# Rotary keys: the weights' high and low parts side by side in one stationary operand, their halves added on VectorE

## The chip, the cores and the metric

One Trainium2 chip, one core of it. A core has TensorE (matrix products into PSUM), VectorE, ScalarE and GpSimd, and 16 DMA engines between HBM and the on-chip SBUF; each engine runs its own list of instructions in order, and they wait for each other on semaphores. The metric is the device time of one execution in microseconds; a kernel's time is the median over its runs.

## The reference

Two blocks on 512 tokens of 1024 channels, in fp32. The first is attention with latent keys, a Fourier branch and experts; the second a recurrent unit and a feed-forward layer. The change touches one small piece of the first block:

```
h  = rms(x, norm1_g) * (1 + sc) + sh          # 512 tokens
hc = rms(ctx, norm1_g) * (1 + csc) + csh      # 256 context tokens
p, pc = h @ w_in, hc @ w_in
k_pe  = p[..., OFF_KPE:OFF_F]                 # 32 rotary columns, one for all heads
k = concat([k_nope, k_pe repeated over heads])
k = rms(k, k_norm_g)                          # mean square over all 96, so k_pe's squares count
k = concat([k[:64], rope(k[64:])])            # latent tokens only
```

So of the 32 rotary key rows three things are wanted: their values, times k_norm_g, and the sum of their squares per token (before k_norm_g).

## The kernel before, in words

Everything is kept with channels on the 128 partitions and tokens along the free axis. Products are made exact enough by splitting each fp32 operand in a high part (fp32r, a rounded copy, made on ScalarE) and a low part (the rest, made on VectorE or, for weights, on GpSimd), and doing three products: high x high, high x low, low x high. That is mm3 (L961 to L963); project (L968) repeats it over the 8 channel blocks of 128. Each such product is one instruction of up to 512 tokens, with its own load of the stationary weights.

Weights come as pieces of 128x2048 through a ring of four raw buffers. ScalarE copies a piece to w_hi (split_weights, L1704, called from take() when the piece is due by the plan), then GpSimd makes w_lo (L895), then the raw buffer is filled again. Three pieces are held in w_hi and w_lo. The weights of the rotary keys, 8 blocks of 32 columns, lie in the third piece of the section "s1".

The order is written out by hand, in one list per engine. PLAN lists the PSUM tiles in the order in which TensorE fills them, with a bank and with who frees each. Around the change, TensorE does:

1. cq and ckv for the 512 tokens (L1078), then rope_rows(0) (L1106): the tile "kpe" 0, 32 rows x 512 tokens, 8 x 3 products;
2. ckv_c for the 256 context tokens (two halves, 48 products), which waits for hc_lo; then rope_rows(1), the tile "kpe" 1, 32 rows x 256;
3. fourier_in(0); then the sums over channels of all squares into the tile ssq_c, as products of one column (L1013 for cq and ckv, L1131 for the rotary keys, the latter after act_seq 3);
4. fourier_in(1); the broadcasts of the inverse norms (L1020); rot_k (L1143), a rotation of the scaled keys, which waits for both "kpe" tiles to be freed; then the rest of the Fourier branch.

ScalarE, in order: hc_hi for 8 blocks (L1714, each waits for VectorE's pre), dftc_hi (L1761), the squares of cq and ckv (L1765), of ckv_c, and of the two "kpe" tiles (L1774, into sqk), then f_hi of the Fourier tiles. VectorE: pre and hc_lo (L2152, L2160), the gains of cq and ckv (L2186, L2201) with the sums of their squares between (L2191), ckv_c, the two "kpe" tiles times k_norm_g into kraw (L2212), f_lo of tile 0 (L2219), then the copy of the key sums (L2222), the inverse norms (L2123 to L2135, some 14 small steps), f_lo of tile 1.

Of the kernel before, what the change touches and what calls it, by code (L numbers as in the profile page):

```python
# [4 lines left out]
F32 = mybir.dt.float32  # L5
F32R = mybir.dt.float32r
I32 = mybir.dt.int32
U32 = mybir.dt.uint32
ALU = mybir.AluOpType
ACT = mybir.ActivationFunctionType  # L10
AX = mybir.AxisListType

P = 128
T = 512
TC = 256
TK = T + TC
D = 1024
KD = D // P
EPS = 1e-6
H = 8  # L20
QK = 96
NOPE = 64
ROPE = 32
VD = 64
QL = 384 // P
KL = 256 // P
# [15 lines left out]
CH = 2048  # L42
NRAW = 4
NHL = 3
# [8 lines left out]
S1_QKV, S1_KPE, S1_F, S1_DFT = 0, 44 * B, 46 * B, 80 * B  # L53
# [28 lines left out]
COLS = {}  # L82
# [102 lines left out]
SPLIT0 = {s: section_start(s, True) for s, _, sp in SECTIONS if sp}  # L185
# [272 lines left out]
PLAN = make_plan()  # L458
TILE = PLAN.tiles
# [29 lines left out]
def build(nc, stream, cols_d, x_d, ctx_d, router_d, wab_d, rope_d, rope_t_d, rot_d, dftc_d, ident_d, iota_d, xt_d, out):  # L489
    with ExitStack() as ctx:  # L490
        base = 16512

        def at(name, kb, shape, dt=F32):
            return nc.alloc_sbuf_tensor_at(name, shape, dt, offset=base + int(kb * 1024))

        def sem(name):
            return ctx.enter_context(nc.semaphore(name))
# [3 lines left out]
        w_hi = at("w_hi", 32, [P, NHL, CH], F32R)  # L501
        w_lo = at("w_lo", 56, [P, NHL, CH], F32R)
        ex_ring = at("ex_ring", 0, [P, NEX - 1, CH])
        R = 80

        x1 = at("x1", R + 96, [P, KD, T])
        cols = at("cols", R + 122.75, [P, NCOLS])
# [35 lines left out]
        ckvg = at("ckvg", R + 54, [P, KL, TK])  # L543
        sq_q = at("sq_cq", R + 60, [P, QL, T])
        sq_kv = at("sq_ckv", R + 66, [P, KL, TK])
# [10 lines left out]
        kraw = at("kraw", R + 104, [QK, TK])  # L556
        sqk = at("sqk", R + 107, [QK, TK])
        rk = at("rk", R + 110, [QK, T])
        rope_t = at("rope_t", R + 112, [P, 2 * TT + 2, ROPE])
        kr_tok = at("kr_tok", R + 113.25, [P, KT, ROPE])  # L560
        rope_cs = at("rope_cs", R + 115, [QK, 2, T])
# [114 lines left out]
        w_lo_done = sem("w_lo_done")  # L676
# [5 lines left out]
        freed_dve = sem("freed_dve")  # L682
# [6 lines left out]
        macc_done = sem("macc_done")  # L689
        modb_done = sem("modb_done")  # L690
        latent_sums = sem("latent_sums")
        modin_full = [sem(f"modin_full{i}") for i in range(KD)]
        x_in = [sem(f"x_in{i}") for i in range(4)]
        ctx_in = sem("ctx_in")
# [3 lines left out]
        sq_done = sem("sq_done")  # L698
# [5 lines left out]
        act_seq = sem("act_seq")  # L704
# [64 lines left out]
        def col(name, j=0, n=1):  # L769
            return cols[:, COLS[name] + j:COLS[name] + j + n]  # L770

        def bank(*name):
            return psum[:, PLAN.bank[TILE[name]], :]

        def full(eng, *name):

# [154 lines left out]
        def _(pe):  # L931
            mm = nc.tensor.matmul
            seen = [0]

            def open_tile(*name):

                t = TILE[name]
                prev = PLAN.prev[t]
                if prev is not None:
                    pe.wait_ge(freeing[PLAN.freed[prev][0]], PLAN.freed_count(prev))  # L940
                return psum[:, PLAN.bank[t], :]
# [23 lines left out]
            def done(ins):  # L965
                ins.then_inc(tile_full, 1)

            def project(o, base, off, width, ks, x_of):  # L968

                for i, k in enumerate(ks):  # L970
                    last = mm3(o, weights(base, off + i * width, width), x_of(k), i == 0, i == len(ks) - 1)
                return last
# [70 lines left out]
            o = open_tile("ssqx_rows")  # L1043
            for j in range(KD):
                pe.wait_ge(sq_done, j // 2 + 1)
                last = row_sums(o, sq_x0, j)
# [6 lines left out]
            o = open_tile("bc_x")  # L1053
# [6 lines left out]
            s1 = SPLIT0["s1"]  # L1060
            hx = lambda k: (h_hi[:, k, :], h_lo[:, k, :])
            hcx = lambda k: (hc_hi[:, k, :], hc_lo[:, k, :])
# [12 lines left out]
            ks = range(KD)  # L1075
# [8 lines left out]
            for k in range(KD):  # L1084
                for i in range(QL + KL):
                    last = qkv_step(i, k)
# [18 lines left out]

            def rope_rows(s):  # L1106

                o = open_tile("kpe", s)
                done(project(o[0:ROPE, 0:TC if s else T], s1, S1_KPE, ROPE, ks, hcx if s else hx))

            rope_rows(0)
            o = open_tile("ckv_c")
# [26 lines left out]
            done(broadcast(o3[2], 2 * TT, 2))  # L1139

            o = open_tile("rot_k")
            pe.wait_ge(freed_dve, PLAN.freed_count(TILE["kpe", 1]))
            done(mm(o[0:QK, :], rotm[NOPE:QK, :], kraw[NOPE:QK, 0:T], start=True, stop=True))  # L1143
            fourier_in(2)
            fourier_in(3)
# [541 lines left out]
        def _(act):  # L1687
# [19 lines left out]
            def take(*name):  # L1707

                split_weights(TILE[name])
                full(act, *name)  # L1710
                return bank(*name)
# [52 lines left out]
            def square(dst, src):  # L1764
                A(dst, src, ACT.Square).then_inc(sq_done, 1)  # L1765

            for j in range(QL):
                square(sq_q[:, j, :], take("cq", j))
            for j in range(KL):
                square(sq_kv[:, j, 0:T], take("ckv", j))  # L1770
            square(sq_kv[:, :, T:TK], take("ckv_c").rearrange("p (j t) -> p j t", j=KL))
            for s in range(2):
                w = slice(T, TK) if s else slice(0, T)
                A(sqk[NOPE:QK, w], take("kpe", s)[0:ROPE, 0:w.stop - w.start], ACT.Square).then_inc(act_seq, 1)  # L1774
            hi(f_hi[:, 0, :], take("f", 0))
            hi(f_hi[:, 1, :], take("f", 1))
            for j in range(QL):
# [282 lines left out]
        def _(dve):  # L2060
# [3 lines left out]
            def link(ins):  # L2064

                n[0] += 1
                ins.then_inc(dve_seq, 1)
                dve.wait_ge(dve_seq, n[0])
# [8 lines left out]
            def take(*name):  # L2077
                full(dve, *name)
                return bank(*name)

            def free(ins):
                ins.then_inc(freed_dve, 1)
# [107 lines left out]
            def latent_sum(dst, src):  # L2190
                V.tensor_tensor(dst, dst, src, ALU.add).then_inc(latent_sums, 1)  # L2191
                sums[0] += 1
                dve.wait_ge(latent_sums, sums[0])
# [6 lines left out]
                dve.wait_ge(sq_done, nsq)  # L2200
                free(V.tensor_scalar(ckvg[:, j, 0:T], o, col("kv_a_norm_g", j), None, ALU.mult))  # L2201
            latent_sum(sq_kv[:, 0, 0:T], sq_kv[:, 1, 0:T])
            o = take("ckv_c")
            dve.wait_ge(sq_done, nsq + 1)
            V.tensor_scalar(ckvg[:, 0, T:TK], o[:, 0:TC], col("kv_a_norm_g", 0), None, ALU.mult)
            free(V.tensor_scalar(ckvg[:, 1, T:TK], o[:, TC:T], col("kv_a_norm_g", 1), None, ALU.mult))
            latent_sum(sq_kv[:, 0, T:TK], sq_kv[:, 1, T:TK])
            for s in range(2):
                w = slice(0, T) if s == 0 else slice(T, TK)
                o = take("kpe", s)  # L2210
                dve.wait_ge(act_seq, 2 + s)
                free(V.tensor_scalar(kraw[NOPE:QK, w], o[0:ROPE, 0:TC if s else T],  # L2212
                                     cols[NOPE:QK, COLS["k_norm_g"]:COLS["k_norm_g"] + 1], None, ALU.mult))
            dve.wait_ge(freed_dve, PLAN.freed_count(TILE["kpe", 1]))

            def evac_lo(dst, hi_part, *name):
                o = take(*name)
                dve.wait_ge(hi_done, SPLITS[name] + 1)
                V.tensor_tensor(dst, o, hi_part.bitcast(F32), ALU.subtract).then_inc(lo_done, 1)  # L2219

            evac_lo(f_lo[:, 0, :], f_hi[:, 0, :], "f", 0)
            link(V.tensor_copy(kpe_s, take("ssq_c")[:, TT + KT:TT + 2 * KT]))  # L2222
            inverse_norms(take("ssq_c"), 10, [(0, 4, 1.0 / (QL * P)), (4, 6, 1.0 / (KL * P))])
            evac_lo(f_lo[:, 1, :], f_hi[:, 1, :], "f", 1)
# [670 lines left out]
```

## Time and profile before

| | us |
|---|---|
| median of 3 runs | 1335.6 |
| lowest, highest | 1334.64, 1336.63 |
| span of the profiled execution | 1332.2 |
| its TensorE busy | 1313.8 |
| its mean granted TensorE clock (share of full speed) | 0.996 |

The profile shows one execution; its span runs from the first to the last instruction, and the profiled execution's own time is not listed apart from it. Times in the trace count from the span's start. In a timeline each row has the start, how long the instruction or a run of them was busy, the engine, the line, output<-input, shapes, and the count; in square brackets how long the engine was idle before it and who released it. "128*32" is a stationary operand of 128 rows and 32 columns. Products are pipelined, so the durations of neighbours overlap: the distance between starts is what one costs.

### The profile page before, as it was taken

The page shows a single profiled execution, that of the slowest core. Times are in us where ns is not written, and L with a number is a line of the kernel's source. Part 1 is how long each engine was busy: PE and PEld are TensorE (multiplying, and loading weights), DVE is VectorE, ACT ScalarE, POOL GpSimd, SP SyncE. Part 2 cuts the span into 40 slices and gives each one's busy share as a digit, 9 for nine tenths or more (in the row PEclk, how much of TensorE's full clock was granted, in tenths as well). Part 3 has the DMA queues.
Part 4 walks back from the last instruction along what each step waited for, and adds up shares of the span by engine and source line. Part 5 has one row for each costly group of instructions (what it writes and reads, how often), then busy time and mean ns, then how long its engine had stood idle before and what let it go on. Part 6 is the DMA issues. An engine that isn't in the chain of part 4 may idle for free.

```text
span 1332.2 us, 15820 instructions
## 1 busy us (share of the span) xinstructions
PE 1313.8 (99%) x6366; PEld 966.9 (73%) x6366; DVE 690.1 (52%) x1261; ACT 461.6 (35%) x618; POOL 433.8 (33%) x136
## 2 busy tenths in 40 slices
PE   8999999999999899999999999999999999999998
PEld 6789888865587834343457788888888888888887
DVE  2465987757783733343356656612562551551553
ACT  4335223345621221121135571433341431431431
POOL 3143244247612000000015333444245344444440
PEclk9999999999999899999999999999999999999999
DMA  9521198201025799999983122222132223123101
GB/s 378 214 96 64 58 356 336 103 1 64 32 96 189 294 375 421 421 421 420 421 367 127 63 80 110 96 95 95 63 126 98 93 95 118 71 94 126 64 1 64
DMA packets 34501, 226.70 MB, mean 170 GB/s; under 512 B 4064, under 2 KB 4704, under 8 KB 8448
## 3 DMA queue, kind: packets, MB, share of 16 engines
q1 hardware_dynamic: 32992, 218.93, 42.9%
q0 software_dynamic: 1152, 4.19, 0.8%
q10 hardware_dynamic: 288, 2.62, 0.5%
q8 instruction: 48, 0.79, 0.2%
q14 instruction: 21, 0.17, 0.0%
HBM read 221.53 MB, written 4.19 MB: 169 GB/s over the span
## 4 chain that ended last, share of the span: by engine, by line
PE 94%; DVE 3%; DMA 1%; ACT 1%; SPq 0%; issue 0%; DVEq 0%; ACTq 0%
PE psum L961 24%; PE psum L963 23%; PE psum L962 23%; PE psum L1465 13%; DMA mod_in<-in_stream 1%; PE psum L1273 1%; PE psum L1239 1%; PE psum L1450 1%; PE psum L1453 1%; PE psum L1008 1%; PE psum L1537 1%; PE psum L1425 1%; PE psum L1674 1%; DVE rs L2381 1%; PE psum L1013 0%; DVE work L2512 0%
## 5 line engine op out<-in xcount | busy, mean ns | idle before, releaser
L895 POOL TENSOR_TENSOR w_lo<-raw,w_hi 128x2048 fp32r<-128x2048 f32 x79 | 365.3, 4627 | 589.9 <-ACT w_hi L1704 589.9
L961 PE MATMUL psum<-b_hi,w_hi 128*128 128x512 f32 x608 | 238.1, 392 | 0.1
L963 PE MATMUL psum<-b_hi,w_lo 128*128 128x512 f32 x608 | 236.7, 389 | 0.0
L962 PE MATMUL psum<-b_lo,w_hi 128*128 128x512 f32 x608 | 236.6, 389 | 0.0
L1704 ACT ACTIVATE w_hi<-raw 128x2048 fp32r<-128x2048 f32 x80 | 152.6, 1907 | 145.4 <-PE psum L963 101.9
L961 PEld LDWEIGHTS psum<-b_hi,w_hi 128*128 128x128 f32 x608 | 114.1, 188 | 30.6 <-issue 5.7
L963 PEld LDWEIGHTS psum<-b_hi,w_lo 128*128 128x128 f32 x608 | 114.1, 188 | 23.9
L962 PEld LDWEIGHTS psum<-b_lo,w_hi 128*128 128x128 f32 x608 | 114.2, 188 | 23.4
L1465 PE MATMUL psum<-ex_ring,xe 128*64 128x512 f32 x488 | 108.8, 595 | 0.9 <-ACT xe L1929 0.9
L2429 DVE TENSOR_TENSOR x<-psum,x 128x512 f32<-128x512 f32 x40 | 27.4, 691 | 124.3 <-PE psum L963 124.3
L961 PE MATMUL psum<-h_hi,w_hi 128*128 128x512 f32 (+1 forms) x208 | 84.7, 407 | 1.3 <-POOL w_lo L878 1.3
L1465 PEld LDWEIGHTS psum<-ex_ring,xe 128*64 128x64 f32 x488 | 34.1, 137 | 66.3 <-issue 65.4
L963 PE MATMUL psum<-h_hi,w_lo 128*128 128x512 f32 (+1 forms) x208 | 81.8, 393 | 0.0
L962 PE MATMUL psum<-h_lo,w_hi 128*128 128x512 f32 (+1 forms) x208 | 81.7, 393 | 0.0
L961 PE MATMUL psum<-ff_hi,w_hi 128*128 128x512 f32 x192 | 74.7, 389 | 0.0
L962 PE MATMUL psum<-ff_lo,w_hi 128*128 128x512 f32 x192 | 74.7, 389 | 0.0
L963 PE MATMUL psum<-ff_hi,w_lo 128*128 128x512 f32 x192 | 74.7, 389 | 0.0
L2710 DVE TENSOR_TENSOR psum<-psum,rstd_s 128x512 f32<-128x512 f32 x48 | 33.5, 697 | 77.4 <-PE psum L963 77.4
L905 POOL DMA_INDIRECT xg<-xt,ids x8 | 8.3, 1040 | 189.6 <-DVE ids L2539 139.0
L2431 DVE SCALAR_TENSOR_TENSOR x<-psum,mod,x 128x512 f32<-128x512 f32 x72 | 51.0, 743 | 25.6 <-PE psum L963 21.0
L1929 ACT ACTIVATE xe<-psum,mod,small 128x128 f32<-128x128 f32 x64 | 23.9, 459 | 83.7 <-PE psum L1425 83.7
L1465 PE MATMUL psum<-ex_ring,act_e 128*64 128x512 f32 x224 | 49.7, 595 | 0.7 <-DVE act_e L2597 0.7
(419 smaller groups left out, 2290.9 us busy)
## 6 DMA issues: line engine op xcount, KB each, us to landing
raw<-in_stream SPq DMA_DIRECT2D x97, 1024.0 KB, 4.8
ex_ring<-in_stream SPq DMA_DIRECT2D x89, 1024.0 KB, 17.7
mod_in<-in_stream SPq DMA_DIRECT2D x8, 1024.0 KB, 21.0
ex_last<-in_stream SPq DMA_DIRECT2D x7, 1024.0 KB
x<-in_x SPq DMA_DIRECT2D x4, 512.0 KB, 6.0
x<-in_x ACTq DMA_DIRECT2D x1, 2048.0 KB, 7.4
xt<-h2t SPq DMA_DIRECT2D x8, 256.0 KB, 11.7
out<-y_out SPq DMA_DIRECT2D x8, 256.0 KB, 3.3
```

The source lines that it names most:

```text
L895: nc.gpsimd.tensor_tensor(w_lo[:, slot, :], raw[:, raw_slot, :], w_hi[:, slot, :].bitcast(F32), ALU.subtract).then_inc(w_lo_done, 1)
L961: mm(o, w[0], x[0], start=start, stop=False)
L962: mm(o, w[0], x[1], start=False, stop=False)
L963: return mm(o, w[1], x[0], start=False, stop=stop)
L1008: mm(psum[:, bank, 0:P], ones[:], ones[:], start=True, stop=True)
L1239: done(mm(o[:, 0:KH], q_hi[b][0:QK, q * P:(q + 1) * P], k_hi[b][0:QK, s * KH:(s + 1) * KH], start=True, stop=True))
L1465: last = mm(o[e * CAP:(e + 1) * CAP, :], x_of(k, e), w[:, (2 * (k - k0) + e) * T:(2 * (k - k0) + e + 1) * T], start=k == 0, stop=k == ks - 1)
L1704: A(w_hi[:, c % NHL, :], raw[:, n % NRAW, :], ACT.Copy).then_inc(w_hi_done, 1)
L1929: ins = A(xe[:, i % 2, k, :], o[:, j * P:(j + 1) * P], ACT.Identity, bias=mod[:, 3 * KD + k, 0:1], scale=a2[:, k:k + 1])
L2429: ins = V.tensor_tensor(x1[:, j, :], o, x1[:, j, :], ALU.add)
L2431: ins = V.scalar_tensor_tensor(out=x1[:, j, :], in0=o, scalar=scale, in1=x1[:, j, :], op0=ALU.mult, op1=ALU.add)
L2710: V.tensor_tensor(o, o, rstd, ALU.mult).then_inc(ffz_done, 1)
```

## The change

The high and the low part of the rotary keys' weights are put side by side in a new buffer w_kpe, 64 columns for each of the 8 blocks, by two copies on ScalarE (kpe_packed counts them). Then two products in place of three do a block: all 64 columns times the high part of x, and times its low part. Rows 0 to 31 of the tile hold what the high weights gave, rows 32 to 63 what the low weights gave; it now holds low x low too. The halves are added on VectorE, after ScalarE has copied the lower one to kraw, and ScalarE takes its squares from the added result. The tiles of "kpe" 0 and ckv_c change places in ScalarE's and VectorE's order. k_norm_g, formerly in the evacuation, becomes one VectorE step over both token sets, behind f_lo of tile 0; rot_k waits for that (kpe_gained).

```
+        w_kpe = at("w_kpe", R + 110, [P, KD, 2, ROPE], F32R)
+        s1_kpe = SPLIT0["s1"] + S1_KPE // CH, S1_KPE % CH
# TensorE
             def rope_rows(s):
-                o = open_tile("kpe", s)
-                done(project(o[0:ROPE, 0:TC if s else T], s1, S1_KPE, ROPE, ks, hcx if s else hx))
+                o = open_tile("kpe", s)[:, 0:TC if s else T]
+                pe.wait_ge(kpe_packed, 2)
+                for k in ks:
+                    both = w_kpe[:, k, :, :].rearrange("p s m -> p (s m)")
+                    x_hi, x_lo = (hcx if s else hx)(k)
+                    mm(o[0:2 * ROPE, :], both, x_hi, start=k == 0, stop=False)
+                    last = mm(o[0:2 * ROPE, :], both, x_lo, start=False, stop=k == KD - 1)
+                done(last)
...
             o = open_tile("rot_k")
-            pe.wait_ge(freed_dve, PLAN.freed_count(TILE["kpe", 1]))
+            pe.wait_ge(kpe_gained, 1)
# ScalarE, behind dftc_hi
+            c, off = s1_kpe
+            act.wait_ge(w_lo_done, c + 1)
+            for part, w in enumerate((w_hi, w_lo)):
+                A(w_kpe[:, :, part, :], w[:, c % NHL, off:off + KD * ROPE].bitcast(F32).rearrange("p (k m) -> p k m", k=KD),
+                  ACT.Copy).then_inc(kpe_packed, 1)
             for j in range(QL):
                 square(sq_q[:, j, :], take("cq", j))
             for j in range(KL):
                 square(sq_kv[:, j, 0:T], take("ckv", j))
-            square(sq_kv[:, :, T:TK], take("ckv_c").rearrange("p (j t) -> p j t", j=KL))
             for s in range(2):
+                if s == 1:
+                    square(sq_kv[:, :, T:TK], take("ckv_c").rearrange("p (j t) -> p j t", j=KL))
                 w = slice(T, TK) if s else slice(0, T)
-                A(sqk[NOPE:QK, w], take("kpe", s)[0:ROPE, 0:w.stop - w.start], ACT.Square).then_inc(act_seq, 1)
+                A(kraw[NOPE:QK, w], take("kpe", s)[ROPE:2 * ROPE, 0:w.stop - w.start], ACT.Copy).then_inc(kpe_low, 1)
+                act.wait_ge(freed_dve, PLAN.freed_count(TILE["kpe", s]))
+                A(sqk[NOPE:QK, w], kraw[NOPE:QK, w], ACT.Square).then_inc(act_seq, 1)
# VectorE
-            o = take("ckv_c")
-            dve.wait_ge(sq_done, nsq + 1)
-            V.tensor_scalar(ckvg[:, 0, T:TK], o[:, 0:TC], col("kv_a_norm_g", 0), None, ALU.mult)
-            free(V.tensor_scalar(ckvg[:, 1, T:TK], o[:, TC:T], col("kv_a_norm_g", 1), None, ALU.mult))
-            latent_sum(sq_kv[:, 0, T:TK], sq_kv[:, 1, T:TK])
             for s in range(2):
+                if s == 1:
+                    o = take("ckv_c")
+                    dve.wait_ge(sq_done, nsq + 1)
+                    V.tensor_scalar(ckvg[:, 0, T:TK], o[:, 0:TC], col("kv_a_norm_g", 0), None, ALU.mult)
+                    free(V.tensor_scalar(ckvg[:, 1, T:TK], o[:, TC:T], col("kv_a_norm_g", 1), None, ALU.mult))
+                    latent_sum(sq_kv[:, 0, T:TK], sq_kv[:, 1, T:TK])
                 w = slice(0, T) if s == 0 else slice(T, TK)
                 o = take("kpe", s)
-                dve.wait_ge(act_seq, 2 + s)
-                free(V.tensor_scalar(kraw[NOPE:QK, w], o[0:ROPE, 0:TC if s else T],
-                                     cols[NOPE:QK, COLS["k_norm_g"]:COLS["k_norm_g"] + 1], None, ALU.mult))
+                dve.wait_ge(kpe_low, 1 + s)
+                free(V.tensor_tensor(kraw[NOPE:QK, w], o[0:ROPE, 0:TC if s else T], kraw[NOPE:QK, w], ALU.add))
...
             evac_lo(f_lo[:, 0, :], f_hi[:, 0, :], "f", 0)
+            dve.wait_ge(act_seq, 3)
+            V.tensor_scalar(kraw[NOPE:QK, :], kraw[NOPE:QK, :],
+                            cols[NOPE:QK, COLS["k_norm_g"]:COLS["k_norm_g"] + 1], None, ALU.mult).then_inc(kpe_gained, 1)
+            dve.wait_ge(kpe_gained, 1)
             link(V.tensor_copy(kpe_s, take("ssq_c")[:, TT + KT:TT + 2 * KT]))
```

## Rows read from the trace of the kernel before

**Rows 1.** The page: span, busy time by engine, and the chain that ended last.
```profile
span 1332.2 us, 15820 instructions
...
PE 1313.8 (99%) x6366; PEld 966.9 (73%) x6366; DVE 690.1 (52%) x1261; ACT 461.6 (35%) x618; POOL 433.8 (33%) x136
...
PE 94%; DVE 3%; DMA 1%; ACT 1%; SPq 0%; issue 0%; DVEq 0%; ACTq 0%
```
**Rows 2.** TensorE's waits, whole span: total us, times, longest; longest first.
```profile
PE psum L1400 <- DVE work L2512: 1.8, 1, 1.8
...
PE psum L961 <- DVE fc_lo L2247: 1.0, 1, 1.0
```
**Rows 3.** Timeline of TensorE, 61.9 to 92.3 us: first product of each tile.
```profile
61.95 0.39 PE L961 MATMUL psum<-h_hi,w_hi 128*32 128x512 f32 x1
...
67.49 0.27 PE L961 MATMUL psum<-hc_hi,w_hi 128*128 128x256 f32 x1
...
73.23 0.28 PE L961 MATMUL psum<-hc_hi,w_hi 128*32 128x256 f32 x1
...
75.97 0.40 PE L961 MATMUL psum<-h_hi,w_hi 128*128 128x512 f32 x1
...
81.43 0.95 PE L1013 MATMUL psum<-ones,sq_cq 128*128 128x1 f32 x8
...
85.67 0.63 PE L962 MATMUL psum<-h_lo,w_hi 128*128 128x512 f32 x1
86.10 0.63 PE L963 MATMUL psum<-h_hi,w_lo 128*128 128x512 f32 x1
...
92.22 2.39 PE L1020 MATMUL psum<-ident,small 128*128 128x128 f32 x20
```
**Rows 4.** Timeline of ScalarE, 65 to 77 us.
```profile
65.37 0.51 ACT L1714 ACTIVATE hc_hi<-pre,mod 128x256 fp32r<-128x256 f32 x1 [0.40 <-DVE pre L2152]
65.78 0.40 ACT L1761 ACTIVATE dftc_hi<-dftc 128x256 fp32r<-128x256 f32 x1
66.09 1.55 ACT L1765 ACTIVATE sq_cq<-psum 128x512 f32<-128x512 f32 x3
...
68.48 1.94 ACT L1704 ACTIVATE w_hi<-raw 128x2048 fp32r<-128x2048 f32 x1
...
76.60 0.37 ACT L1774 ACTIVATE sqk<-psum 32x256 f32<-32x256 f32 x1
```
**Rows 5.** Timeline of VectorE, 71 to 88 us.
```profile
71.56 4.10 DVE L2191 TENSOR_TENSOR sq_ckv<-sq_ckv 128x512 f32<-128x512 f32 x1
...
76.94 1.13 DVE L2212 TENSOR_SCALAR kraw<-psum,cols 32x512 f32<-32x512 f32 x2
82.36 0.69 DVE L2219 TENSOR_TENSOR f_lo<-psum,f_hi 128x512 fp32r<-128x512 f32 x1 [4.29 <-ACT f_hi L1714]
85.19 0.17 DVE L2222 COPY small<-psum 128x6 f32<-128x6 f32 x1 [2.14 <-PE psum L1131]
...
87.88 0.17 DVE L2135 SCALAR_TENSOR_TENSOR small<-psum,small 128x10 f32<-128x10 f32 x1
```
**Rows 6.** Timeline of GpSimd, 30 to 75 us.
```profile
34.65 4.59 POOL L895 TENSOR_TENSOR w_lo<-raw,w_hi 128x2048 fp32r<-128x2048 f32 x1 [6.09 <-ACT w_hi L1704]
...
70.50 4.62 POOL L895 TENSOR_TENSOR w_lo<-raw,w_hi 128x2048 fp32r<-128x2048 f32 x1 [31.27 <-ACT w_hi L1704]
```
**Rows 7.** Two windows: length, busy us (instructions) by engine, granted clock, DMA, GB/s.
```profile
81.60:85.00 3.40, 3.40 (x31) 3.38 (x31) 0.69 (x1) 2.40 (x2) 0.90 (x1) 1.00 0.80 246
85.00:88.40 3.40, 3.40 (x10) 2.71 (x10) 2.42 (x14) 0.00 (x0) 3.40 (x1) 0.50 0.16 65
```
**Rows 8.** The same for two windows in the routing stage.
```profile
453.60:457.00 3.40, 2.23 (x17) 1.89 (x17) 1.99 (x8) 0.00 (x0) 0.00 (x0) 1.00 1.04 401
457.00:463.90 6.90, 6.90 (x32) 6.73 (x33) 5.71 (x23) 0.00 (x0) 2.69 (x2) 0.51 0.44 128
```
**Rows 9.** Groups by line and form on VectorE: busy us, mean ns, idle before.
```profile
L2729 DVE TENSOR_SCALAR diag_g<-ident,cols 128x128 f32<-128x128 f32 x8 | 6.1, 837 | 0.0
```

More of the change, by code:

```diff
@@ L691, in build @@
         latent_sums = sem("latent_sums")
+        kpe_packed = sem("kpe_packed")
+        kpe_low = sem("kpe_low")
+        kpe_gained = sem("kpe_gained")
         modin_full = [sem(f"modin_full{i}") for i in range(KD)]
```

## The prediction

> **What bounds the kernel now.** I read the page first: TensorE is busy 1313.8 of 1332.2 us, and 94% of the chain that ended last is TensorE's own work [rows 1]. So a change pays or costs what it does to TensorE's stream. The list of TensorE's waits comes next: each one is under 2 us in 1332 us, so no engine or transfer paces TensorE over a long stretch; the nearest one behind this change is 1.0 us, for fc_lo in the Fourier branch [rows 2]. Then I went to the place itself, TensorE's timeline from 61.9 us on [rows 3]. "kpe" 0 begins at 61.95, ckv_c at 67.49, "kpe" 1 at 73.23, fourier_in(0) at 75.97, the sums of squares at 81.43, and TensorE has no gap between them. In the same stretch I read when ScalarE is free [rows 4], because the change gives ScalarE work that TensorE must wait for; then VectorE and GpSimd [rows 5, 6], whose steps around the keys are changed; last TensorE's granted clock [rows 7, 8], because the change opens a hole in TensorE's stream.
>
> The sum is made against the profiled execution, span 1332.2 us; its own time is not given apart from the span. The three timed runs have a median of 1335.6 us, 3.4 above it (what lies before the first and after the last instruction, 2.4 to 4.4 in single runs). I take that rest as unchanged and put the difference on the median.
>
> **Part 1, fewer products.** Each "kpe" tile has 8 steps of three products; after the change it has 8 steps of two. "kpe" 0 takes 67.49 - 61.95 = 5.54 us for 24 products, 0.231 each; "kpe" 1 takes 75.97 - 73.23 = 2.74 us for 24, 0.114 each [rows 3]. Eight products less in each: -1.85 and -0.91, together -2.76 us, all on TensorE's path. Does a product with 64 stationary columns cost more than one with 32? Nothing in this stretch has 64, but fourier_in(0), with 128 columns, takes 81.43 - 75.97 = 5.46 us for 24, 0.228 each, the same as with 32. Between two equal ends I take no extra.
>
> **Part 2, the packing, and TensorE's wait for it.** TensorE now waits, before "kpe" 0, for two copies on ScalarE. What they read is long there (GpSimd's product for the third piece, in which these weights lie, started at 34.65 and took 4.59 us [rows 6]). What is late is their turn: they stand in ScalarE's order behind all eight hc_hi and behind dftc_hi. The last hc_hi starts at 65.37 (each waits for VectorE's pre), dftc_hi at 65.78, and the next instruction starts at 66.09 [rows 4]. dftc_hi has the size of a packing copy, 128x256 from SBUF to SBUF: 0.40 us, the next one starting 0.31 after it. So the copies start at 66.09 and 66.40 and end at 66.80; with a handover TensorE starts at about 66.9. By the neighbour of equal size, hc_hi at 0.51, and without overlap, it would be 67.2. TensorE wants to start "kpe" 0 at 61.95. **The wait costs 66.9 - 61.95 = 4.95 us** (bounds 4.8 and 5.3), and nothing covers it: all that TensorE has to do stands behind the waiting product, ckv_c among it, whose operands hc are ready only when this wait is nearly over (the hc_lo of the last hc_hi follows 65.9).
>
> Sum so far: 4.95 - 1.85 - 0.91 = **+2.2 us**.
>
> **Part 3, the clock.** TensorE's granted clock is 1.00 (2.4 GHz) through this stretch. Where TensorE streamed nearly nothing it fell: the sums of squares (products of one column) run from 81.43, and in 85.0 to 88.4 the clock is 0.50 (1.2 GHz) [rows 7]; products start 0.43 us apart there (85.67, 86.10) instead of 0.228 [rows 3]. A second place is softer: from 453.6 to 457.0 TensorE was still busy 2.23 of 3.40 us, much of it with tiny products, and the next 6.9 us were at 0.51 [rows 8]. The new hole is 4.95 us with no product at all, emptier than both, so I expect the clock to fall. The half-speed stretch of 3.4 us holds 3.4/0.43 = 8 products in place of 15, which costs 3.4 x (1 - 0.228/0.43) = 1.6 us. The hole is longer than that stretch, so part of the fall can pass unused inside the hole (about 0.9 us lost then), or it lasts until 4.5 us after the resumption (2.1 us lost, half of 4.5 with rounding). I take **+1.6 us**; bounds 0.9 and 2.2. The fall at the sums of squares is there already, costs the same 1.6 us and moves along with them: no difference taken, give or take 0.5.
> The Trainium skill ("TensorE: Matmul & The Clock Gate", "What's actually happening") has the throttled clock as the default that activity releases, which speaks against a change that empties TensorE; by it the sum is the one with this term, and without it the sum would stay at +2.2. The two falls in this trace agree with it.
>
> **Part 4, the longer evacuation.** Before, each "kpe" tile had one square on ScalarE and one scaling on VectorE. Now: copy of the low half (ScalarE), add (VectorE), square (ScalarE), and one scaling of 32x768 on VectorE later. Let TensorE's shift be 3.8 us up to 4.2 at this point. "kpe" 1 is then complete at about 80.2. Behind it on ScalarE stands a weight split (1.94, as at 68.48) begun at about 79.2, so the copy starts at 81.1 and takes 0.4, the add 0.5 (the 256-wide part of the 1.13 at 76.94 [rows 5]), the square 0.37 [rows 4]: 82.5. The first sums that need it come at 81.43 + 4 = 85.4 at the earliest. Covered by 2.9 us of fourier_in(0). If ScalarE's queue were later by more than that, TensorE would wait for the difference.
> "kpe" 0 needs the VectorE queue, and there the sum of ckv's squares took 4.10 us at 71.56 [rows 5], although one of this size takes 0.69 (f_lo at 82.36): it ended 0.54 after GpSimd's product (70.50 + 4.62 = 75.12 [rows 6]). With ScalarE's squares 0.6 later, so is the product (71.1 to 75.7) and so is this end (76.3); add and square of "kpe" 0 follow to 77.6. ckv_c is not complete before 78, so nothing is held up.
>
> **Part 5, the scaling in its own step.** It stands behind the f_lo of tile 0 (82.36, 0.69) and before the copy of the key sums at 85.19, which VectorE reached with 2.14 us idle [rows 5]. Shifted: f_lo ends at about 87.2, the sums arrive at 89.3. The scaling costs at most the 1.13 of its two former pieces: hidden in that idle time. If it falls together with a product on GpSimd it may be stuck like the 4.10 above: diag_g, scalings of 128x128 that should be short, average 0.837 [rows 9]. The next product begins about 1 us after the scaling should have (GpSimd starts such a product 1.9 us behind the ScalarE split, which itself follows f 0). If it is stuck for all of it, up to 5.4 us, VectorE reaches the norms 4 us late. That cover is the stretch between the end of the norms (87.88 + 0.17 = 88.05) and the broadcasts of them on TensorE (92.22 [rows 3]): 4.2 us. So it costs 0, at worst 0.3. rot_k's new wait for the scaling stands behind these broadcasts: 0. Here the Trainium skill ("SBUF — State Buffer", the part on the shared port pair) says that the pair is locked for a whole instruction against a VectorE operation with two SBUF inputs or in a two-port mode. The row of 4.10 agrees; the sum is the same either way.
>
> No DMA is issued by the change. The refills of the weight ring follow GpSimd's products, here 0.6 us up to 4 us later, and no wait of TensorE for them stands in [rows 2].
>
> **Sum.** +4.95 - 2.76 + 1.6 = **+3.8 us**, 1335.6 + 3.8 = **1339.4 us**. Bounds: 4.8 - 2.76 + 0.9 = +2.9, and 5.3 - 2.76 + 2.2 + 0.3 = +5.0.
>
> **Rivals.** (a) The hole does not pull the clock down, or later stages give a part back: +2.2, 1337.8 us. For it: the wait for fc_lo [rows 2], 1.0 us, could take up part of the delay if the other engines' work there were not moved along; against it, that work follows TensorE's own tiles, and the hole is emptier than both stretches after which the clock fell. (b) The clock falls for as long as at 457 us, 6.9 us, of which about 6.5 behind the hole: 6.5 x 0.47 = 3.1 in place of 1.6, so +5.3, 1340.9 us. For it: VectorE, ScalarE and TensorE are all late together here; against it, dense products follow the hole at once, as at 85 us, where 3.4 us sufficed. (c) The other side: the copies are not in TensorE's way. If ScalarE could do them in the gaps of 0.40 us between its hc_hi, all before 61.95, the change would be its saving alone: -2.76, 1332.8 us. It decides at 61.95 + 2.76 = 64.7: copies done before that make it faster, later ones slower. The gaps exist (0.40 us idle before the hc_hi at 65.37 [rows 4]), but ScalarE works in the order of its program, and that has the copies last.
>
> **How the numbers follow.** Forecast 0.69; (a) 0.19; (b) 0.08; (c) 0.04. What this kernel's timing can tell from no change is 0.2%, 2.7 us. The forecast's own bounds, +2.9 to +5.0, lie above it, as does (b); I leave 0.04 of the forecast's share to the spread of medians. (a) lies within. Slower 0.73, the same 0.23, faster 0.04. Range: from +1.5 (holds (a) with its spread) to +5.6 (holds (b)): 1337.1 to 1341.2.
>
> **What would show it.** In the profile after: TensorE's first "kpe" product near 66.9 with a wait of almost 5 us for ScalarE's w_kpe, at the top of TensorE's waits; 16 products in each tile, 0.23 and 0.115 apart at full clock; a stretch of 3.4 us at 0.50 beginning in or just behind the hole; ckv_c about 5 us later, the broadcasts about 4 us later than 92.22; no wait of TensorE at the sums of squares. I am wrong if "kpe" 0 starts before 64.7, if products of 64 columns are spaced wider, or if the clock stays at 1.00.

## The result, and the profile after

| | before | after |
|---|---|---|
| median | 1335.8 us (8 runs) | 1340.05 us (8 runs) |
| lowest, highest | 1333.07, 1337.31 | 1335.12, 1341.65 |
| span of the profiled execution | 1332.2 | 1339.3 |
| mean granted TensorE clock in it | 0.996 | 0.990 |

The ratio is 1.0029 [1.0016, 1.0043], or +3.9 us on 1335.8 (+2.1 to +5.7). It is formed from all runs, so it isn't quite the quotient of the medians, which are 4.25 us apart; where a gain is given "in the runs" below, it goes by the ratio. The forecast was +3.8. A second set of runs of the changed kernel (e7 below) gave 1.0029 [1.0018, 1.0041]. The two profiled executions are 7.1 us apart. The one of after took 1341.08 us, 1.8 more than its span and 1.0 above its median; with the same 1.8, the one of before took 1334.0, which is 1.8 below its median. That leaves 7.1 - 1.0 - 1.8 = 4.3 between the medians. So the two profiles are from different ends of their spreads.

The page of after, the lines that answer to [rows 1]: still a chain of TensorE's own work.
```profile
span 1339.3 us, 15796 instructions
...
PE 1316.7 (98%) x6350; PEld 969.3 (72%) x6350; DVE 690.4 (52%) x1262; ACT 463.5 (35%) x622; POOL 433.5 (32%) x136
...
PE 94%; DVE 3%; DMA 1%; ACT 1%; issue 0%; SPq 0%; DVEq 0%; ACTq 0%
```
TensorE has 16 products less than before and is busy 2.9 us longer: products got slower. The list of its waits [rows 2] has a new head:
```profile
PE psum L1119 <- ACT w_kpe L1782: 4.8, 1, 4.8
```
The timeline of TensorE after, 62 to 99 us, for [rows 3]:
```profile
67.59 0.66 PE L1119 MATMUL psum<-h_hi,w_kpe 128*64 128x512 f32 x1 [4.83 <-ACT w_kpe L1782]
68.04 0.63 PE L1120 MATMUL psum<-h_lo,w_kpe 128*64 128x512 f32 x1
...
72.64 0.39 PE L1119 MATMUL psum<-h_hi,w_kpe 128*64 128x512 f32 x1
72.87 0.40 PE L1120 MATMUL psum<-h_lo,w_kpe 128*64 128x512 f32 x1
...
73.56 0.28 PE L967 MATMUL psum<-hc_hi,w_hi 128*128 128x256 f32 x1
...
79.32 0.28 PE L1119 MATMUL psum<-hc_hi,w_kpe 128*64 128x256 f32 x1
...
81.14 0.40 PE L967 MATMUL psum<-h_hi,w_hi 128*128 128x512 f32 x1
...
86.61 0.95 PE L1019 MATMUL psum<-ones,sq_cq 128*128 128x1 f32 x8
...
90.80 0.80 PE L967 MATMUL psum<-h_hi,w_hi 128*128 128x512 f32 x1
...
99.00 2.39 PE L1026 MATMUL psum<-ident,small 128*128 128x128 f32 x20
```
The first product of "kpe" 0 stands 4.83 us for w_kpe. The first products behind it start 0.43 us apart, those from 72.64 on 0.23: the clock changed in between. ScalarE's timeline in the same stretch shows why TensorE stood [rows 4]:
```profile
66.02 0.51 ACT L1726 ACTIVATE hc_hi<-pre,mod 128x256 fp32r<-128x256 f32 x1 [0.41 <-DVE pre L2172]
66.43 0.40 ACT L1773 ACTIVATE dftc_hi<-dftc 128x256 fp32r<-128x256 f32 x1
66.74 0.40 ACT L1782 ACTIVATE w_kpe<-w_hi 128x256 fp32r<-128x256 f32 x1
67.04 0.40 ACT L1782 ACTIVATE w_kpe<-w_lo 128x256 fp32r<-128x256 f32 x1
```
The copies come last and end at 67.44. Four windows of after (length, busy us and instructions of TensorE, its weight loads, VectorE, ScalarE, GpSimd, then granted clock, DMA share, GB/s), to hold against [rows 7]:
```profile
62.60:65.70 3.10, 0.15 (x1) 0.00 (x0) 2.96 (x8) 1.80 (x4) 0.00 (x0) 1.00 0.00 0
65.70:72.50 6.80, 4.91 (x12) 2.71 (x13) 5.87 (x11) 5.65 (x10) 0.75 (x1) 0.50 0.00 0
86.60:89.60 3.00, 3.00 (x28) 2.98 (x27) 1.30 (x2) 2.51 (x2) 0.32 (x2) 1.00 0.58 177
89.60:96.40 6.80, 6.80 (x20) 5.67 (x20) 2.42 (x14) 0.00 (x0) 4.35 (x1) 0.50 0.41 133
```
Some 3 us into the hole the clock falls from 2.4 to 1.2 GHz for 6.8 us, of which 1.9 lie in the hole and 4.9 behind it. The fall behind the sums of squares, 3.4 us long before, lasts 6.8 here too.

To see where the time went, I measured each tile from its first product to the first of the next, in every profile but those of e6 and e9, where the order of the tiles or of the sums is another. The first column is the distance from the broadcast bc_c (58.06 before, 58.71 after) to "kpe" 0, so it holds the hole; the last is the sum, up to the broadcasts of the norms.

| us | to kpe 0 | kpe 0 | ckv_c | kpe 1 | fourier 0 | sums | fourier 1 | sum |
|---|---|---|---|---|---|---|---|---|
| before | 3.89 | 5.54 | 5.74 | 2.74 | 5.46 | 3.65 | 7.14 | 34.16 |
| after | 8.88 | 5.97 | 5.76 | 1.82 | 5.47 | 4.19 | 8.20 | 40.29 |
| e7, after again | 8.88 | 5.61 | 5.75 | 1.83 | 5.47 | 4.57 | 7.83 | 39.94 |
| e1, copies early | 3.88 | 3.68 | 5.76 | 1.82 | 6.18 | 3.70 | 7.10 | 32.12 |
| e2, hole filled | 8.79 | 3.73 | 5.75 | 1.83 | 5.46 | 3.64 | 7.13 | 36.33 |
| e3, wait only | 8.87 | 7.36 | 5.75 | 2.74 | 5.47 | 4.03 | 8.35 | 42.57 |
| e4, third product | 3.87 | 5.53 | 5.75 | 2.73 | 5.46 | 4.35 | 8.06 | 35.75 |
| e5, copies midway | 5.83 | 3.70 | 5.76 | 1.82 | 5.47 | 4.41 | 8.00 | 34.99 |
| e8, e1 + early split | 3.88 | 3.68 | 5.76 | 1.82 | 5.74 | 3.64 | 7.21 | 31.73 |

The 7.1 us between the two profiles are: 6.13 in these tiles, 0.65 from a later start (58.71 against 58.06, so from ahead of the changed code; over all profiles bc_c starts between 58.06 and 58.91), and 0.3 behind. The stage behind the norms' broadcasts, up to the query projection, is 33.42 us long in both.

### The profile page after: what moved, and what is told of

Same layout as the page of the kernel before. It is cut to its first block, busy times and chain, and to the rows that moved or that the text cites. A ratio compares the mean times of both kernels' runs of the same rounds, so it can differ in the third digit from the quotient of the medians.

```text
span 1339.3 us, 15796 instructions
## 1 busy us (share of the span) xinstructions
PE 1316.7 (98%) x6350; PEld 969.3 (72%) x6350; DVE 690.4 (52%) x1262; ACT 463.5 (35%) x622; POOL 433.5 (32%) x136
## 3 DMA queue, kind: packets, MB, share of 16 engines
q0 software_dynamic: 1152, 4.19, 0.8%
HBM read 221.53 MB, written 4.19 MB: 169 GB/s over the span
## 4 chain that ended last, share of the span: by engine, by line
PE 94%; DVE 3%; DMA 1%; ACT 1%; issue 0%; SPq 0%; DVEq 0%; ACTq 0%
PE psum L967 23%; PE psum L969 23%; PE psum L968 23%; PE psum L1477 13%; DMA mod_in<-in_stream 1%; PE psum L1285 1%; PE psum L1251 1%; PE psum L1462 1%; PE psum L1465 1%; PE psum L1549 1%; PE psum L1437 1%; PE psum L1686 1%; PE psum L1014 1%; DVE rs L2405 1%; PE psum L1019 0%
## 5 line engine op out<-in xcount | busy, mean ns | idle before, releaser
L967 PE MATMUL psum<-h_hi,w_hi 128*128 128x512 f32 x200 | 81.9, 410 | 1.3 <-POOL w_lo L884 1.3
L969 PE MATMUL psum<-h_hi,w_lo 128*128 128x512 f32 x200 | 79.1, 396 | 0.0
L968 PE MATMUL psum<-h_lo,w_hi 128*128 128x512 f32 x200 | 79.0, 395 | 0.0
```

Of the source, the lines that this page charges most:

```text
L967: mm(o, w[0], x[0], start=start, stop=False)
L968: mm(o, w[0], x[1], start=False, stop=False)
L969: return mm(o, w[1], x[0], start=False, stop=stop)
```

## The experiments

My theory: the packing copies stand last in ScalarE's order and open a hole of 5 us; the hole pulls the clock down; the product saving is real and the longer evacuation is free. Against it: 64 columns or the evacuation cost the time, or the hole alone without the clock.

**e1, the copies early.** The packing block is moved ahead of the eight hc_hi.
```
             A(sum_c[:], take("ssqc_rows")[:, 0:TC], ACT.Copy).then_inc(freed_act, 1)
+            c, off = s1_kpe
+            act.wait_ge(w_lo_done, c + 1)
+            for part, w in enumerate((w_hi, w_lo)):
+                A(w_kpe[:, :, part, :], w[:, c % NHL, off:off + KD * ROPE].bitcast(F32).rearrange("p (k m) -> p k m", k=KD),
+                  ACT.Copy).then_inc(kpe_packed, 1)
             for j in range(KD):
                 hi_of_pre(hc_hi[:, j, :], pre[:, j % 2, 0:TC], bias=mod[:, j, 1:2])
...
-            c, off = s1_kpe
-            act.wait_ge(w_lo_done, c + 1)
...
```


> The changed kernel with the two packing copies moved forward in ScalarE's order, ahead of the eight hc_hi (ScalarE idles 6 us there). My theory: the loss is the wait for late copies and the clock fall that the empty stretch brings, and the products saved are a true gain. Then kpe 0 starts without a wait at about 62, no fall of the clock at 65 to 72 us, and the time is 2.8 us under the kernel before (ratio 0.9979). Rival 1, the longer evacuation (copy, add, square, scaling) costs the time: still slower than before, +1 us or more. Rival 2, 64 columns make products dearer: no gain, ratio 1.000, with kpe products spaced wider than 0.23 us.

Measured: 0.9975 [0.9963, 0.9986], 1332.0 us (11 runs) against 1335.7 (28). TensorE's timeline in e1:
```profile
62.79 0.40 PE L1119 MATMUL psum<-h_hi,w_kpe 128*64 128x512 f32 x1
...
76.01 0.50 PE L967 MATMUL psum<-h_hi,w_hi 128*128 128x512 f32 x1 [0.41 <-POOL w_lo L901]
```
No wait at "kpe" 0, and 5.54 - 3.68 = 1.86 and 2.74 - 1.82 = 0.92 us saved in the two tiles, as forecast. Against the changed kernel it is 0.54% or 7.2 us less, and the only edit is the place of two copies of 0.4 us. The second row is what became late next: fourier_in(0) reaches its third block before GpSimd has its low weights, and loses 0.7 us of the 2.8.

**e2, the hole filled.** The changed kernel, with idle products of ones into the tile's own bank ahead of the wait.
```
                 o = open_tile("kpe", s)[:, 0:TC if s else T]
+                if s == 0:
+                    idle_products(20, PLAN.bank[TILE["kpe", 0]])
                 pe.wait_ge(kpe_packed, 2)
```


> The changed kernel with the wait kept, but TensorE streams 20 products of ones (4.4 us of work, results thrown away) ahead of it. My theory: the wait stays at about 5 us in all, the clock stays at 1.00 behind it and the 1.6 to 2.3 us that the fall cost come back: +2.2 us against before (ratio 1.0016), kpe 0 takes 3.7 us and not 6.0. Rival: the fall is not due to the empty stretch (it comes with a time or with the load of the other engines): the clock falls all the same and the time stays at +3.9 us or above.

Measured: 1.0017 [1.0007, 1.0026], 1337.71 us. TensorE's timeline and two windows of e2:
```profile
62.70 4.62 PE L1014 MATMUL psum<-ones 128*128 128x128 f32 x40
67.61 0.45 PE L1121 MATMUL psum<-h_hi,w_kpe 128*64 128x512 f32 x1 [0.28 <-ACT w_kpe L1784]
```
```profile
62.60:67.60 5.00, 4.73 (x42) 4.50 (x40) 4.57 (x11) 3.38 (x9) 0.00 (x0) 1.00 0.00 0
67.60:71.30 3.70, 3.69 (x16) 2.26 (x17) 3.10 (x5) 3.70 (x6) 0.00 (x0) 1.00 0.00 0
```
"kpe" 0 starts at the same time as in the changed kernel, but the clock stays at 1.00 and the tile takes 3.73 us in place of 5.97. So the hole costs in two ways, and the clock's part is 2.2 us in the trace; in the runs it is 0.12%, 1.6 us, with intervals that overlap.

**e3, the wait without the saving.** The kernel before, with w_kpe, both copies and the wait in rope_rows; three products a block and the old evacuation stay.
```
             def rope_rows(s):
                 o = open_tile("kpe", s)
+                pe.wait_ge(kpe_packed, 2)
                 done(project(o[0:ROPE, 0:TC if s else T], s1, S1_KPE, ROPE, ks, hcx if s else hx))
...
```


> The kernel before with nothing but the packing copies on ScalarE and TensorE's wait for them; the three products per block and the old evacuation stay. My theory: the full price of the wait and the fall without the saving, +4.95 +1.6 to 2.3 = +6.5 to +7.3 us (ratio 1.005), and 2.8 us above the changed kernel. Rival (the wait is cheap and the new evacuation order is what costs): +2 us or less.

Measured: 1.0060 [1.0048, 1.0072], 1344.25 us (6 runs), +8.0, which is above the +6.5 to +7.3 that was expected; the interval, +6.4 to +9.6, takes that in. Timeline of TensorE and a window of e3:
```profile
67.71 0.61 PE L965 MATMUL psum<-h_hi,w_hi 128*32 128x512 f32 x1 [4.83 <-ACT w_kpe L1775]
```
```profile
64.90:71.70 6.80, 3.99 (x10) 1.71 (x11) 5.83 (x12) 6.07 (x11) 0.00 (x0) 0.50 0.00 0
```
The same hole and the same fall without any product of 64 columns. In its profile the price is 42.57 - 34.16 = 8.41 us: hole 4.98, "kpe" 0 at half clock 1.82, and 1.6 at the sums, whose fall was the long one. The expectation had not counted the last.

**e4, the third product put back.** e1, with eight extra products per tile that are overwritten, so that each tile has 24 again.
```
+                for k in ks:
+                    mm(o[0:2 * ROPE, :], w_kpe[:, k, :, :].rearrange("p s m -> p (s m)"), (hcx if s else hx)(k)[0],
+                       start=True, stop=True)
                 for k in ks:
                     both = w_kpe[:, k, :, :].rearrange("p s m -> p (s m)")
```


> As the kernel with the copies moved forward, but with a third product per block put back, whose result is overwritten: 24 products per kpe tile as before, with the new evacuation. My theory: TensorE's stream is as long as before and the evacuation is hidden: 0 against before (within 0.1%), 2.8 us above the kernel with the copies moved forward. Rival (the gain or loss comes from the evacuation or from the changed order on ScalarE and VectorE): it differs from before by over 1.5 us.

Measured: 0.9996 [0.9985, 1.0007], 1336.18 us (12 runs). With the copies early and 24 products a tile, the new evacuation, the added step and the packing cost nothing that can be told (the interval is -2.0 to +0.9 us); and what e1 has more, 0.21% or 2.8 us, is the 2.76 us of the sixteen products. Its two windows around the sums:
```profile
81.40:84.80 3.40, 3.40 (x30) 3.27 (x28) 1.88 (x2) 2.67 (x3) 3.40 (x2) 1.00 0.01 2
84.80:91.60 6.80, 6.80 (x21) 5.67 (x22) 2.83 (x15) 0.00 (x0) 4.80 (x1) 0.50 0.59 182
```
The long fall at the sums is here although TensorE has no hole and no fall before it.

**e5, the copies midway.** The packing block between the fifth and the sixth hc_hi.
```
                 hi_of_pre(hc_hi[:, j, :], pre[:, j % 2, 0:TC], bias=mod[:, j, 1:2])
+                if j == 4:
+                    c, off = s1_kpe
+                    act.wait_ge(w_lo_done, c + 1)
...
```


> The changed kernel with the two packing copies between the fifth and the sixth hc_hi on ScalarE, so that they end some 1.8 us after TensorE wants kpe 0, in place of 4.95. My theory: a hole of about 1.8 us, too short to pull the clock down, so -2.8 +1.8 = -1.0 us against before (ratio 0.9993, between 0.998 and 1.000), kpe 0 at 3.7 us. Rival: any hole brings the fall of the clock, +1.6 more: ratio 1.0005 and products 0.43 us apart behind it.

Measured: 0.9984 [0.9972, 0.9995], 1334.04 us against 1335.73. TensorE's timeline and the window around it:
```profile
64.60 0.41 PE L1119 MATMUL psum<-h_hi,w_kpe 128*64 128x512 f32 x1 [1.79 <-ACT w_kpe L1776]
```
```profile
61.00:68.30 7.30, 5.51 (x24) 3.41 (x24) 6.88 (x16) 5.28 (x13) 0.00 (x0) 1.00 0.00 0
```
A hole of 1.79 us brings no fall: "kpe" 0 takes 3.70 us. The two tiles save 2.76, the hole takes 5.83 - 3.89 = 1.94, which leaves 0.8 us; the runs say 2.1 (interval 0.7 to 3.7). In its own profile that gain doesn't show: the fall at the sums was the long one, which cost 1.6.

**e6, other work in the hole.** ckv_c ahead of "kpe" 0 in TensorE's order and in the plan, and in ScalarE's and VectorE's order; the copies stay last.
```
...
-            rope_rows(0)
             o = open_tile("ckv_c")
...
             done(last)
+            rope_rows(0)
             rope_rows(1)
...
```


> The changed kernel with ckv_c ahead of both kpe tiles on TensorE (and in ScalarE's and VectorE's order), so that its products, which follow hc_lo one by one, fill the stretch in which the copies are awaited. My theory: TensorE has 21 products of ckv_c (2.5 us) to do before the last hc_lo at about 67, the second half of ckv_c behind it, and the copies are ready by then: no wait for w_kpe, about 2 us of short holes for hc_lo, no fall of the clock; -2.8 +2.0 = -0.8 us against before (ratio 0.9994). Rival (the wait for the copies is only renamed into a wait for hc_lo of the same length): +2 us or more.

Measured: 0.9997 [0.9988, 1.0006], 1335.22 us. TensorE's timeline in e6:
```profile
64.10 0.39 PE L967 MATMUL psum<-hc_hi,w_hi 128*128 128x256 f32 x1 [0.29 <-DVE hc_lo L2179]
...
69.91 0.39 PE L1119 MATMUL psum<-h_hi,w_kpe 128*64 128x512 f32 x1
...
81.31 1.02 PE L1019 MATMUL psum<-ones,sq_cq 128*128 128x1 f32 x8 [0.28 <-DVE sq_ckv L2210]
```
The wait for w_kpe is gone, and the clock stays up, but ckv_c now runs at the pace at which its operands hc come (blocks at 63.18, 64.10, 65.01 and 65.92, 0.91 apart; 0.36 at full pace) and takes 69.91 - 62.08 = 7.83 us instead of 5.75. That is 2.1 of the 2.8 us saved. Another 0.45 goes behind fourier_in(0), of which 0.28 is the wait for ckv_c's squares, and 0.4 in the sums (85.37 - 81.31 = 4.06). The hole was cut in pieces, not removed.

**e7, the changed kernel again**, without an edit: does its profile show the same each time?

> The changed kernel once more, on this chip and beside the others. My theory: +3.9 us (ratio 1.0029) and again a fall of the clock right behind the wait for w_kpe, of 3.4 or 6.8 us in this profile, while the fall at the sums of squares may be of either length. Rival (the profile of the changed kernel, 7.1 us longer in its span than the one before, is the true difference): ratio 1.005.

Measured: 1.0029 [1.0018, 1.0041], 1340.56 us (12 runs). Ten runs are at 1339.9 to 1341.4 us with a mean clock of 0.989 to 0.992, two at 1335.9 with 0.996; in the eight runs of after, too, two stand apart (1335.12 and 1336.08, clock 0.996). The profiled one (1340.98) has the fall in the hole at 64.9, 6.8 us long.

**e8, e1 with the next weights split earlier**, against e1's wait for w_lo.
```
             for j in range(QL):
                 square(sq_q[:, j, :], take("cq", j))
+            split_weights(TILE["kpe", 0])
             for j in range(KL):
```


> The kernel with the copies moved forward (e1_hoist), and the next weight split (third ring piece after these) one place earlier on ScalarE, ahead of the two squares of ckv. With the stall gone, fourier_in(0) waited 0.41 us for that piece's w_lo on GpSimd in e1_hoist, and its products with it took 0.7 us longer in all than before. My theory: the split starts at 68.4 in place of 69.3, w_lo is ready 0.9 us earlier and the wait is gone: 0.4 to 0.7 us under e1_hoist, -3.2 to -3.5 us against before by the traces (ratio 0.9973). Rival: GpSimd or the refill is what is late, and the wait stays at 0.4.

Measured: 0.9969 [0.9957, 0.9982], 1330.71 us (9 runs) against 1334.9 (14). The row of TensorE that answers to the wait of e1, and GpSimd's product:
```profile
75.38 0.50 PE L967 MATMUL psum<-h_hi,w_hi 128*128 128x512 f32 x1
```
```profile
70.17 5.16 POOL L901 TENSOR_TENSOR w_lo<-raw,w_hi 128x2048 fp32r<-128x2048 f32 x1 [30.33 <-ACT w_hi L1716]
```
The wait is gone and the tile takes 5.74 us in place of 6.18, where before it took 5.46: GpSimd's product took 5.16 us in place of the 4.61 of e1, and ended 0.6 us earlier, not 0.9. 0.4 us is below what the medians of e1 and e8 can tell apart, but this has the lowest ratio of all, 4.1 us under before.

**e9, the sums among dense products.** e8, with the one-column sums two behind each of the first eight products of fourier_in(1), against the fall that every version has at the sums.
```
...
+                for i, (a, b) in enumerate(((w[0], x[0]), (w[0], x[1]), (w[1], x[0]))):
+                    last = mm(o1, a, b, start=k == 0 and i == 0, stop=k == KD - 1 and i == 2)
+                    for n in range(2):
+                        m = 2 * (3 * k + i) + n
+                        if m < len(sums):
+                            dst, sta, mov = sums[m]
+                            s = mm(dst, sta, mov, start=m == 0, stop=True, skip_group_check=True)
...
```


> e8_early with the 16 one-column sums of ssq_c set between the first eight products of fourier_in(1), two behind each, in place of a block of 3.65 us ahead of them. My theory: the fall of the clock behind the sums, 3.4 us in the kernel before and 6.8 in the changed one, comes from that block and is what spreads the medians; spread out, no fall at 80 to 92 us, fourier_in(1) and sums together 9.1 us (5.46 + 3.65) in place of 10.8 to 12.4: 1.6 to 3.2 us under e8_early (ratio about 0.996). Rival: one-column products cost the same as before wherever they stand and pull the clock down all the same, or the norms on VectorE come too late for the broadcasts: no gain.

Measured: 1.0026 [1.0014, 1.0039], 1337.9 us (7 runs): a miss. TensorE's timeline and two windows of e9:
```profile
80.96 0.47 PE L1147 MATMUL psum<-h_hi,w_hi 128*128 128x512 f32 x1 [1.59 <-ACT sqk L1804]
```
```profile
81.00:82.70 1.70, 1.70 (x13) 1.58 (x13) 1.09 (x2) 1.68 (x2) 1.70 (x1) 1.00 0.02 5
82.70:96.40 13.70, 13.70 (x44) 10.95 (x43) 4.18 (x15) 0.68 (x1) 6.13 (x2) 0.51 0.45 153
```
The fall came anyway and lasted 13.7 us, four times as long as the 3.4 of e8. And since the wait for the last squares now stands ahead of the first sum, 1.59 us of it came to light that the sums of cq and ckv had covered. Wait, sums and fourier_in(1) take 1.59 + 97.12 - 80.96 = 17.75 us against 10.85 in e8, most of the 7.6 us between the two in the runs. The fall begins at 83.0 (the second window starts 0.3 us ahead of it, hence its 0.51), 1.7 us after the first sum, but 3.6 us after that wait began, so the mixing alone isn't shown to bring it: a version without the wait was not run. VectorE's scaling, 0.61 us in the changed kernel, fell together with GpSimd's work here (two products from 79.51 to 88.84):
```profile
82.30 2.17 DVE L2253 TENSOR_SCALAR kraw<-kraw,cols 32x768 f32<-32x768 f32 x1
```

## Why the prediction was right, and what was off in it

**The bound and the products.** TensorE's stream decides, as said. The saving is 1.86 and 0.92 us at full clock (forecast 1.85 and 0.91), and e4 prices it at 2.8 us in the runs. Products with 64 columns are 0.23 and 0.114 us apart, like those with 32 or 128.

**The hole.** Forecast 4.95 us, measured 8.88 - 3.89 = 4.99, and 4.98 in e3. The reason is the one read from [rows 4]: the copies are short, only their turn is late. e1 shows it by changing nothing but the turn, and e5 lies in between, where a hole of 1.94 is less than what the products save, as the point of 64.7 us in rival (c) has it. That rival fails because ScalarE works in its program's order, not because the gaps are missing.

**The clock: the term that was mis-sized.** The forecast took a fall of 3.4 us at a price of 1.6 (0.9 to 2.2). All three profiles with the 5 us hole (after, e3, e7) have one of 6.8 us. After: 4.9 us of it behind the hole, 4.9 x (1 - 0.228/0.43) = 2.3 us; e7 1.93 by "kpe" 0's length (5.61 - 3.68), e3 1.82 (7.36 - 5.54). I took the length from [rows 7] where [rows 8] had the right one; rival (b) had that length, but put only 0.4 us of it into the hole instead of 1.9 to 2.8, so it came out too high. The upper bound of 2.2 rested on 4.5 us of fall behind the hole, which a fall of 3.4 us can't give and no row of before showed; 4.9 us came. What settles how much is lost is when in the hole the fall begins, and that no row of before could tell. The Trainium skill ("TensorE: Matmul & The Clock Gate", "What's actually happening") has the half clock as what idleness leads to, with sustained activity as the way back, at a point that varies from run to run. The traces agree: the clock fell at 65.7 in one execution of the changed kernel and at 64.9 in the other, and was back at 72.5 and at 71.7, 4.9 and 4.1 us after the first product behind the hole. Its sentence that the ramp is under 1% and need not be fitted holds here for the size (2.3 of 1340 us), but it is more than half of what this change does.

**The fall at the sums.** "Moves along, give or take 0.5" failed in the profile: it was 6.8 us in place of 3.4 and cost 0.54 in the sums and 1.06 in fourier_in(1), 1.6 together. Is that the change's doing? e4 and e5 have the long fall without any fall before it; before, e1, e2, e6 and e8 have the short one; after, e3 and e7 the long one. So the hole isn't needed for it. The same ten profiles (e9 apart) show what goes with the length: where the fall is long it begins 2.6 to 3.2 us after the first sum (after 89.6 - 86.6), with 0.9 to 2.0 us of the sums still to run; where it is short, 3.5 to 4.5 us after it (before 85.0 - 81.4), with 0.3 us of them left or none. There is no exception among the ten. No run sets where it begins, so the reason for that stays open, and so does whether the hole makes the long one more likely: it came in 3 of 3 profiles with the open hole of 5 us and in 2 of the other 7.

**The sum.** With what lies in place, the change is 4.99 - 2.78 + 2.3 = +4.5 us; the runs say +3.9 (2.1 to 5.7) and the forecast was +3.8. With the clock's term 0.7 us too small, that forecast and ratio meet within 0.1 us is luck; that they meet within the interval is not. The four runs of twenty at 1335.1 to 1336.1 us with clock 0.996 pull the ratio down. By my estimate from the mean clock they have about 11 us at 1.2 GHz (1336 x 2 x 0.004) and the other sixteen 21 to 29, so they lack more than one fall of 6.8 us; which ones is not known, as none of them was profiled. The routing stage varies too: its falls sum to 6.8 us in before, e1, e2, e6 and e9, with 1238.9 to 1240.0 us from the norms' broadcasts to the end of the span, and to 10.2 or 13.7 in the others, with 1240.3 to 1241.4.

Of the signs that the forecast named, the wait, its place at the top, the spacings and no wait at the sums are there. ckv_c came 6.1 us later instead of 5 and the broadcasts 6.8 instead of 4: 0.65 of both is the later start; the rest is the longer fall behind the hole, and for the broadcasts the one at the sums as well. The forecast's rest of 3.4 us outside the span was wrong: it is 1.8 to 1.9 in every profile that has both numbers, and the profiled execution of before was a quick one. As the difference went on the median, that moved nothing.

**The evacuation and the scaling: hidden, as said.** ScalarE's and VectorE's rows of after around "kpe" 1, and VectorE's at the norms, to hold against [rows 5]:
```profile
82.08 0.38 ACT L1792 ACTIVATE kraw<-psum 32x256 f32<-32x256 f32 x1
83.04 0.41 ACT L1794 ACTIVATE sqk<-kraw 32x256 f32<-32x256 f32 x1 [0.58 <-DVE kraw L2233]
```
```profile
72.81 4.10 DVE L2211 TENSOR_TENSOR sq_ckv<-sq_ckv 128x512 f32<-128x512 f32 x1
76.94 0.68 DVE L2233 TENSOR_TENSOR kraw<-psum,kraw 32x512 f32<-32x512 f32 x1
...
88.26 0.61 DVE L2243 TENSOR_SCALAR kraw<-kraw,cols 32x768 f32<-32x768 f32 x1
90.98 0.17 DVE L2246 COPY small<-psum 128x6 f32<-128x6 f32 x1 [2.11 <-PE psum L1143]
```
The squares are done at 83.45 (forecast 82.5), the sums start at 86.61: 3.2 us of cover (forecast 2.9). The keys' own sums, which alone need them, start later still, at 88.8. The scaling took 0.61, and VectorE was idle for 2.11 us behind it; it was not stuck behind GpSimd, whose product starts at 89.42. In e1, e4, e5, e8 and e9, where it fell together with one, it took 1.60 to 2.17, within the forecast's bound of 5.4, and TensorE waited for nothing behind it. The 4.10 row is there as before. (The forecast has GpSimd's product 1.9 us behind the split; the rows, 68.48 and 70.50, give 2.0. Nothing hangs on it.) e4 prices the whole at nothing, give or take 2 us.

## What to carry to other kernels

A setup copy that the pacing engine must wait for is priced by its place in its engine's list, not by its length: two copies of 0.4 us cost 7 us where they stood last, and nothing ahead of the eight instructions that each wait for another engine. Read, for each new wait, when the producer's engine gets to it, and what a hole of that length does to the clock behind it. And when a saving on the pacing engine is real, look at once for what is late next (here weights due 0.4 us after TensorE now wants them).

## What the runs showed of the hardware

- Ten profiles of nearly the same code have the fall at the sums at 3.4 or 6.8 us, with 1.6 us between them. The length goes with where in the sums the fall begins. A difference of one profile against one, below some 3 us here, is no evidence.
- A hole of 1.79 us in TensorE's stream (e5), and three of 0.29 us in a row (e6), left the clock at 2.4 GHz; holes of 4.83 us (after, e3, e7) took it to 1.2 GHz some 2 to 3 us after they had begun. Idle products of 128 columns in the hole kept it up (e2).
- The clock falls behind a stretch of one-column products in which TensorE counts as busy for 3.40 of 3.40 us [rows 7]. With the same sums set two behind each of eight dense products, and a wait of 1.59 us just ahead, the clock fell 1.7 us after the first of them and stayed down for 13.7 us (e9); which of the two brought that is not shown.
